# The last feed-forward output as seven block products, with sums made on GpSimd

## The reference, cut to what matters

```python
def swiglu(h, w_in, w_out):
    gate, up = jnp.split(h @ w_in, 2, axis=-1)
    return (jax.nn.silu(gate) * up) @ w_out          # (512, 2816) @ (2816, 1024)

def residual_post_norm(x, y, gate, weight, gain, bias):
    return layer_norm(DN_ALPHA * x + weight * gate[:, None, :] * y, gain, bias)

x = residual_post_norm(x, swiglu(modulate(x, m, 2), ffn2_w_in, ffn2_w_out), m[:, 8], FFN_HALF, ln_gain[2], ln_bias[2])
```

## Time and profile before

| | |
|---|---|
| median of 3 runs | 1345.9 us |
| the profiled execution, its span (first to last instruction) | 1344.9 us |
| the median of the runs over that span | 1.0 us |
| matmuls | 7200 |
| busy share of TensorE, VectorE, ScalarE, GpSimd | 98%, 60%, 38%, 6% |
| mean granted clock of TensorE, as a share of full | 0.995 |

### The profile page before, as it was taken

The page is one execution under the profiler, slowest core; times in us unless marked ns, Lnnn a source line. Parts: engine busy times, 40 slices in busy tenths (PEclk is TensorE's granted clock), DMA queues, the critical chain, the costliest instruction groups (busy, mean ns, idle before and its releaser), DMA issues.

```text
span 1344.9 us, 17714 instructions
## 1 busy us (share of the span) xinstructions
PE 1323.4 (98%) x7200; PEld 1116.1 (83%) x7200; DVE 801.2 (60%) x1146; ACT 517.5 (38%) x718; POOL 74.2 (6%) x83
## 2 busy tenths in 40 slices
PE   8999999999999999999999999999999999999997
PEld 5778888888889999888888788887898888888886
DVE  5546588666777776565136878777863333433356
ACT  5535211222213544566235655556652231222211
POOL 1000000000000000000001111110000000000000
PEclk8999999999999999999999999999999999999999
DMA  9965545665455676552022112123335333333211
GB/s 319 285 177 175 195 151 157 190 186 180 151 178 147 190 188 189 173 172 94 23 79 64 48 48 63 48 64 114 107 85 159 94 103 97 96 101 105 86 63 63
DMA packets 206400, 175.00 MB, mean 130 GB/s; under 512 B 6906, under 2 KB 175464, under 8 KB 206320
## 3 DMA queue, kind: packets, MB, share of 16 engines
q1 hardware_dynamic: 197816, 142.74, 36.6%
q0 software_dynamic: 7808, 29.46, 6.6%
q10 hardware_dynamic: 696, 1.68, 0.4%
HBM read 171.74 MB, written 2.11 MB: 129 GB/s over the span
## 4 chain that ended last, share of the span: by engine, by line
PE 89%; DVE 5%; ACT 3%; issue 2%; DMA 1%; ACTq 0%; DVEq 0%; SPq 0%
PE ps L1962 28%; PE ps L1964 27%; PE ps L1963 27%; PE ps L2001 1%; DVE w_lo L1291 1%; PE ps L2413 1%; PE ps L2398 1%; DMA w_raw<-ffn_w_in 1%; PE ps L2161 0%; PE ps L2014 0%; PE ps L2432 0%; PE ps L2184 0%; DVE xl L1384 0%; DVE xl L1433 0%; PE ps L2205 0%
## 5 line engine op out<-in xcount | busy, mean ns | idle before, releaser
L1962 PE MATMUL ps<-h_hi,w_lo 128*128 128x512 f32 (+1 forms) x1120 | 391.4, 349 | 2.1 <-DVE h_lo L1584 1.0
L1964 PE MATMUL ps<-h_hi,w_hi 128*128 128x512 f32 (+1 forms) x1120 | 387.8, 346 | 0.0
L1963 PE MATMUL ps<-h_lo,w_hi 128*128 128x512 f32 (+1 forms) x1120 | 387.6, 346 | 0.0
L1291 DVE TENSOR_TENSOR w_lo<-w_raw,w_hi 128x2048 fp32r<-128x2048 f32 (+1 forms) x107 | 237.1, 2218 | 169.8 <-ACT w_hi L839 169.7
L839 ACT ACTIVATE w_hi<-w_raw 128x2048 fp32r<-128x2048 f32 (+1 forms) x107 | 198.3, 1854 | 344.9 <-PE ps L1964 315.4
L1962 PEld LDWEIGHTS ps<-h_hi,w_lo 128*128 128x128 f32 x1120 | 211.7, 189 | 32.5 <-issue 5.3
L1964 PEld LDWEIGHTS ps<-h_hi,w_hi 128*128 128x128 f32 x1120 | 211.7, 189 | 26.9
L1963 PEld LDWEIGHTS ps<-h_lo,w_hi 128*128 128x128 f32 x1120 | 211.8, 189 | 25.5
L1313 DVE SCALAR_TENSOR_TENSOR ada_row<-ada_block,c_cols,ada_row 128x256 f32<-128x256 f32 x224 | 108.6, 485 | 8.0
L1462 DVE TENSOR_TENSOR glu<-ps,glu 128x512 f32<-128x512 f32 (+1 forms) x66 | 39.4, 598 | 123.0 <-ACT glu L899 123.0
L1962 PE MATMUL ps<-h_hi,half_lo 128*128 128x512 f32 (+1 forms) x272 | 102.0, 375 | 0.7 <-ACT beside_lo L1123 0.4
(11 more groups left out here) (273 smaller groups left out, 1770.9 us busy)
## 6 DMA issues: line engine op xcount, KB each, us to landing
w_raw<-ffn_w_in SPq DMA_DIRECT2D x124, 512.0 KB, 5.3
w_raw<-ffn_w_out SPq DMA_DIRECT2D x60, 512.0 KB, 4.2
ada_block<-w_ada POOLq DMA_DIRECT2D x28, 1024.0 KB, 5.8
half_raw<-w_mix_in SPq DMA_DIRECT2D x48, 256.0 KB, 3.3
ada_block<-w_ada SPq DMA_DIRECT2D x6, 1024.0 KB, 9.5
w_raw<-ffn_w_in SPq DMA_DIRECT2D x32, 128.0 KB, 6.1
w_raw<-w_mix_in SPq DMA_DIRECT2D x8, 512.0 KB, 4.2
w_raw<-ffn_w_out SPq DMA_DIRECT2D x12, 256.0 KB, 4.1
```

Of the source, the lines that this page charges most:

```text
L1291: nc.vector.tensor_tensor(lo, raw, hi.bitcast(F32), ALU.subtract).then_inc(s_lo[s], 1)
L1962: nc.tensor.matmul(dst, s_low, m_high, start=start, stop=False)
L1963: nc.tensor.matmul(dst, s_high, m_low, start=False, stop=False)
L1964: return nc.tensor.matmul(dst, s_high, m_high, start=False, stop=stop)
```

## The change

The output is a product of 2 x 2 blocks by 2 x 2 blocks: tokens in two halves of 256, the 22 k-tiles in two halves of 11, output columns in two halves of 512. It is made with seven block products (P1 to P7) in place of eight. With left blocks A00, A01, A10, A11 (token half, k half) and weight blocks B00, B01, B10, B11 (k half, column half) the order is P1, P5, P3, P6, P2, P7, P4. Right operands: P1, P3, P2 use B00, B11, B10 as loaded; P5 = B01 + B00, P6 = P5's + B11, P4 = P6's + B10 (`WEIGHT_SUMS`); P7 = B01 + B11. Signs lie in the left operands, sums and differences of token blocks.

- The hidden rows are kept unsplit in `hid_last` (22 x 512 float32); the network has one part of 22 hidden tiles. Each left operand is split when used, by 3 steps of 4, 4, 3 k-tiles a product, into three small slots: `left_high` on ScalarE, `left_low` on VectorE, 256 columns a k-tile.
- GpSimd makes the left sums (11 of 256 columns during the hidden tiles, then 9 steps `left_n2`, `left_s4`, `left_s3`, in place) and the 9 weight sums (`add_beside`), all by `tensor_tensor` from SBUF to SBUF. A raw buffer of P1, P3, P2 is free only when its sum is made too.
- B01 for P5 is loaded on its own by SyncE (`upper_right`), the first step early, the other two after the last hidden product.
- P7's weights: B01 is loaded by SyncE, then GpSimd issues a load of B11 that adds into the same buffer (`add_lower_right`), step s waiting for the high part of step s - 1.
- P1, P6, P7, P4 add up in the same two banks, P5 and P3 in two others. ScalarE copies the banks of P1, P5 and P3 out (`keep`); VectorE joins them with later banks (`join`), multiplies by the gate row and adds to the residual (`add_joined`). P4's first matmul of a tile waits for P7's join of that tile.
- The weights of the last half are not gated any more; the last addition has the gate product ahead of it. The last product has a `LAST_ORDER` of its own.
- Elsewhere several semaphores are merged (the exponentials of the decays into one; the scan mask with the ones; the waits of ScalarE on itself).

```diff
-FFN_PARTS = {"L1": (11, 11), "C": (22,), "L2": (11, 11)}
+FFN_PARTS = {"L1": (11, 11), "C": (22,), "L2": (22,)}
+SEVEN = ("P1", "P5", "P3", "P6", "P2", "P7", "P4")
+SEVEN_STEPS = (4, 4, 3)
+LAST_ORDER = [(0, 0), (0, 1), (1, 0), (2, 0), (1, 1), (2, 1)]
...
             def load(i, pieces=2):
-                if i >= 2:
-                    sp.wait_ge(s_lo[slot_of(i - 2)], USES[i - 2] + 1)
+                before = RAW_USERS[RAW_TURN[i] - 2]
+                sp.wait_ge(s_lo[slot_of(before)], USES[before] + 1)
+                if JOBS[before][1:2] == ("seven",) and JOBS[before][2] in ADDED_BESIDE:
+                    sp.wait_ge(s_wsum, sums_made(*JOBS[before][2:]))
...
+                if key == ("L2", "in", 0, 12):
+                    sp.wait_ge(s_h, PRE["lat", 2, TL - 1] + 1)
+                    upper_right(0)
+                if key == ("L2", "seven", "P1", 1):
+                    last = JOB["L2", "in", 0, 21]
+                    sp.wait_ge(s_done[slot_of(last)], USES[last] + 1)
+                    upper_right(1)
+                    upper_right(2)
...
+            def add_beside(p, s):
+                i = JOB["L2", "seven", p, s]
+                pool.wait_ge(s_loaded[raw_slot(i)], 32 * raw_loads(i))
+                if p == "P1":
+                    pool.wait_ge(s_x[min(s, 1)], 48 if s else 32)
+                else:
+                    split = JOB["L2", "seven", "P5" if p == "P3" else "P6", s]
+                    pool.wait_ge(s_lo[slot_of(split)], USES[split] + 1)
+                    pool.wait_ge(s_wsum, sums_made(p, s) - 3)
+                nc.gpsimd.tensor_tensor(weight_sums[s], weight_sums[s], weights(i)[0], ALU.add).then_inc(s_wsum, 1)
...
+            def left_s4(s):
+                pool.wait_ge(s_left, left_sums("P6", s))
+                pool.wait_ge(s_leftlo, seven_number("P5", s) + 1)
+                nc.gpsimd.tensor_tensor(left("P3", s), left("P2", s), left("P6", s), ALU.subtract).then_inc(s_left, 1)
...
+            def add_lower_right(s):
+                i, (k0, kk) = JOB["L2", "seven", "P7", s], seven_k(s)
+                if s:
+                    pool.wait_ge(s_hi[slot_of(i - 1)], USES[i - 1] + 1)
+                pool.wait_ge(s_loaded[raw_slot(i)], 32 * raw_loads(i))
+                pool.dma_start(weights(i)[0], w2o[:, 11 + k0:11 + k0 + kk, W:D], accum_op=ALU.add).then_inc(s_wacc, 16)
+
+            for j in range(11):
+                pool.wait_ge(s_hf, HID["L2", 0, 11 + j] + 1)
+                nc.gpsimd.tensor_tensor(hid_last[:, j, 256:512], hid_last[:, j, 256:512], hid_last[:, 11 + j, 256:512],
+                                        ALU.subtract).then_inc(s_left, 1)
+            for s in range(3):
+                add_beside("P1", s)
+                left_n2(s)
+            for s in range(3):
+                left_s4(s)
+            for s in range(3):
+                add_beside("P3", s)
+                left_s3(s)
+            add_beside("P2", 0)
+            add_beside("P2", 1)
+            add_lower_right(0)
+            add_beside("P2", 2)
+            add_lower_right(1)
+            add_lower_right(2)
...
+            def left_high(p, s):
+                n = seven_number(p, s)
+                if n == 2:
+                    wait_done(JOB["L2", "in", 0, 21])
+                if n >= 3:
+                    wait_done(SEVEN_FIRST + n - 3)
...
+                for n in range(3 * len(SEVEN)):
+                    p, s = JOBS[SEVEN_FIRST + n][2:]
+                    if n in (3, 6, 9):
+                        keep(SEVEN[n // 3 - 1], 1)
+                    split_both_hi(n + 2)
+                    if n in (2, 5, 8):
+                        keep(p, 0)
...
+            def left_low(p, s):
+                n = seven_number(p, s)
+                dve.wait_ge(s_lefthi, n + 1)
+                hi, lo = left_slot(p, s)
+                nc.vector.scalar_tensor_tensor(out=lo, in0=left(p, s), scalar=left_sign(p), in1=hi.bitcast(F32), op0=ALU.mult,
+                                               op1=ALU.subtract).then_inc(s_leftlo, 1)
...
+                for n in range(3 * len(SEVEN)):
+                    p, s = JOBS[SEVEN_FIRST + n][2:]
+                    before = SEVEN[n // 3 - 1]
+                    if s == 0 and before in ("P6", "P2", "P7") and n:
+                        join(before, 1)
+                        add_joined(before, 1)
+                    split_both_lo(n + 2)
+                    if s == 2 and p in ("P6", "P2", "P7"):
+                        join(p, 0)
+                        add_joined(p, 0)
+                    if n == 16:
+                        for i in range(2):
+                            post_center("lat", 2, i)
+                    if n == 18:
+                        for i in range(2):
+                            post_scale("lat", 2, i)
...
+            def seven_free(p, tile):
+                if p in ("P6", "P3"):
+                    pe.wait_ge(s_kept, (2 if p == "P3" else 0) + tile + 1)
+                if p in ("P7", "P4"):
+                    pe.wait_ge(s_joined, (4 if p == "P4" else 0) + tile + 1)
```

More of the change, by code:

```diff
@@ L8 @@
+import itertools
 from contextlib import ExitStack
@@ L99, in slot_of, with loads_raw @@
     return ((L2_FIRST + 1) % 2, L2_FIRST % 2, 2)[(i - L2_FIRST - 1) % 3] if i > L2_FIRST else 3
+def loads_raw(i):
+    return not (JOBS[i][1:2] == ("seven",) and JOBS[i][2] in WEIGHT_SUMS)
+RAW_USERS = [i for i in range(len(JOBS)) if loads_raw(i)]
+RAW_TURN = {i: n for n, i in enumerate(RAW_USERS)}
+SEVEN_FIRST = JOB["L2", "seven", SEVEN[0], 0]
 USES = [sum(slot_of(j) == slot_of(i) for j in range(i)) for i in range(len(JOBS))]
@@ L146, in out_keys @@
 def out_keys(tag):
+    if tag == "L2":
+        return [(tag, 0, half, i) for half, tiles in ((1, (0, 1)), (0, (0, 1)), (1, (2, 3)), (0, (2, 3))) for i in tiles]
     tiles = TC if tag == "C" else TL
@@ L639, in load @@
                     return
+                if key[1:2] == ("seven",):
+                    (row, half), (k0, kk) = SEVEN_LOADED[key[2]], seven_k(key[3])
+                    for a, b in ((0, 2), (2, kk)):
+                        sp.dma_start(raw[:, a:b, :], w2o[:, 11 * row + k0 + a:11 * row + k0 + b, half * W:(half + 1) * W]
+                                     ).then_inc(s_loaded[s], 16)
+                    return
                 if key[1:2] == ("out",):
@@ L1260, in _ @@
                 high_part(PRE["lat", 2, i])
-            ffn("L2")
-            nc.scalar.preload_act_table_set("sqrt_and_others")
-            for i in range(TL):
-                std_of("post", "lat", 2, i, i + 1)
+            last_ffn()
         @block.vector
@@ new lines, in product_done, with join @@
+            def product_done(p, tile):
+                if tile:
+                    wait_done(JOB["L2", "seven", p, 2])
+                else:
+                    dve.wait_ge(s_seven, SEVEN.index(p) + 1)
+            def join(p, tile):
+                early = {"P6": "P3", "P2": "P1", "P7": "P5"}[p]
+                product_done(p, tile)
+                dve.wait_ge(s_kept, 2 * ("P1", "P5", "P3").index(early) + tile + 1)
+                y = early_sum[early, tile]
+                nc.vector.tensor_tensor(y, y, seven_bank(p, tile), ALU.add if p == "P2" else ALU.subtract
+                                        ).then_inc(s_joined, 1)
@@ L2122, in ffn, with last_ffn @@
+            def last_ffn():
+                for j in range(3, 22):
+                    hidden("L2", 0, j, 0, SEQ)
+                    between("L2", j)
+                for p in SEVEN:
+                    for s, tile in LAST_ORDER if p == SEVEN[-1] else itertools.product(range(3), range(2)):
+                        seven_products(p, s, tile)
             def ffn(tag):
@@ L2131, in ffn @@
                     for half in range(2):
[L2132 to L2135 removed]
+                        b = out_half(tag, part, half, b)
             def between(tag, b):
```

332 lines of the change are left out of this document (223 added, 109 removed).

## The result

The changed kernel took 1389.2 us, the median of 4 runs from 1388.35 to 1390.42; the kernel before, on the same chip, 1345.8 us (4 runs, 1345.26 to 1345.98). The ratio is 1.0323, with an interval from 1.0309 to 1.0338: slower by 43 us. The forecast was 1380, with 1362 to 1400 as the likeliest case and rival B taken in down to 1345.

The account below looks back on a forecast made before the run. TensorE's matmuls were taken to bound the kernel. The terms -15.0 + 27.3 + 14.2 + 5.9 + 1.6 gave +34.0 us on a span of 1344.9, plus 1.0 for the median: 1380, likeliest 1362 to 1400, range down to 1345.

Parts of the forecast that it names:

- rival B: Seven products: exclusion does not hold at these sizes or GpSimd yields; +5 us, 1351, or 1345; chance 0.18.
- rival A: Seven products: the main forecast, GpSimd and VectorE excluding each other plus slow adding loads; 1362 to 1400; chance 0.52.
- rival D: TensorE's clock: stalls between bursts could bring half speed, adding 5 to 20 us, 1385 to 1400; chance 0.14.
- Matmuls, -15.0: Last network's output on TensorE: 462 matmuls in place of 528, same form, 104.7 us for 119.7; gain 15.0 us.
- The exclusion, +27.3: Hidden products' end to P6's last step: GpSimd's sums and VectorE's low parts alternate, stalling TensorE 27.3 us.
- The rate of 2.04 ns a column for GpSimd: GpSimd's two-input sums: rate taken from its 512-column operation, giving 4.18 us for 2048 columns.
- The term without exclusion: P1's third step: late even without exclusion, ready at 14.2 us where TensorE wants it at 10.9; 3.5 us.
- The adding load, +14.2: P7's weights: adding loads taken at 8 us (6 for the third) make its steps 5.8, 5.6 and 2.8 us late.
- P4, +5.9: Before P4: its first matmul waits for VectorE's join of P7, queued behind low parts and post-centres; 5.9 us late.
- the tail, +1.6: After the last matmul: gate product ahead of the last addition, 0.70 us, and VectorE's previous tile 0.9; +1.6 us.
- C: Seven products: no exclusion and an adding load under 4.5 us, started early; -6 us, 1340; chance 0.14.
- The row that spoke for B: Profile before: VectorE's subtraction took 1.23 us beside GpSimd's one-input form, which did not lengthen it.

Follow-up runs that it names:

- e1: Changed kernel with each of GpSimd's 18 sums after the hidden tiles replaced by two fills of its destination, reading nothing: 1365.9 us, ratio 1.0144.
- e7: Kernel before with twelve two-input additions and five one-input products added on GpSimd in the last network, nothing depending on them: 1346.3 us, ratio 0.9999.
- e3: Changed kernel with a semaphore for each adding load, which no longer waits for the previous step's high part: 1390.3 us, ratio 1.0324.
- e5: e3 with GpSimd's last sum with P2's weights before the first adding load, and VectorE's P7 joins ahead of low parts: 1386.3 us, ratio 1.0303.
- e4: Changed kernel with GpSimd's 18 sums after the hidden tiles cut to one column, waits and signals kept: 1361.1 us, ratio 1.0107.
- e8: e6 with the orders of e9 and the nine later left sums moved from GpSimd to VectorE: 1359.9 us, ratio 1.0102.
- e10: e8 with the last three adding loads (P4's weights) replaced by GpSimd additions, and a semaphore for each load of B01: 1365.6 us, ratio 1.0142.
- e9: e6 with P4's adding loads behind P7's, P6's joins around low parts, and output work behind the next low parts: 1364.3 us, ratio 1.0138.
- e6: Changed kernel reordered P1, P5, P3, P6, P7, P2, P4; P6's and P4's weight sums by adding loads, own semaphores, earlier first sum and P6 join: 1359.3 us.

## Why the prediction was right, and where it was short

The sum was +34.0 us on the span; it is 1388.0 - 1344.9 = +43.1. The mechanisms of rival A came, and half clock, which was rival D, came on top of them; the size and its parts, term by term:

- **Matmuls, -15.0.** Right: 7134 of them, at the same pace wherever the clock was full.
- **The exclusion, +27.3.** Right in kind (e1, e7) and near in size. The prediction added up the two engines' work and had P6,2 start 83.1 us after the last hidden matmul; it started at about 84. What the prediction took for stalls alone is 19.6 us of stalls and 8.6 us of the rest, some 6.4 of it at half clock. That the two engines set the pace of this stretch fits GpSimd's timeline, which from 1218.8 to 1283.0 us stands still for 1.0 us in all; that a TensorE at full clock would only have waited longer was not tested. The rate of 2.04 ns a column for GpSimd was low: the first two additions of 2048 columns in the changed kernel, for which it hardly waited, took 4.61 and 4.52 us, 4.18 was taken, and the means are 5.1 to 5.2, with the waiting for VectorE inside. The term without exclusion was added up wrongly: 6.4 + 4.2 + 1.5 + 1.8 is 13.9 and not 14.2, so P1,2 late by 3.0 (e1: 3.2); nothing hangs on it.
- **The adding load, +14.2.** 15.3 measured (6.9, 6.7 and 1.7 for 5.8, 5.6 and 2.8). That they come so near is in part luck. The load's time was mis-sized, 9.5 and 7.7 us where 8 and 6 were taken, inside the bounds of 5.8 and 11.6. And one step of the chain was wrong: P7,1 was put down to the load that waits for the high part of P7,0. By e3 that wait costs P7,1 nothing; it waited for its own plain load, whose buffer was held by GpSimd's sum with P2,2's weights, queued behind a wait. The prediction had not asked what stands behind that wait on GpSimd.
- **P4, +5.9, and the tail, +1.6.** 5.6 and 1.3 (8.9 against 7.6). e5, where the join was moved, took the stall to 2.3, which fits the queue as the prediction had it.
- **The clock.** This is the term that was short: half clock stood at nothing in the sum, as rival D with 0.14, and it came on top of A. D's 1385 to 1400 holds the measured time. The seven stretches hold 34.1 us; with the restarts, TensorE's matmuls took 16.7 us more than at the hidden tiles' pace. Of these 8.6 lie up to P6,2, inside the term above, the other 8 beside P7 and P4. With them the sum is -15.0 + 28.2 + 15.3 + 5.6 + 8.0 + 1.3 = +43.4. That 1380 came within 9 us owes something to luck, since half of what the clock took fell where the prediction had waiting already.
- **The rivals.** B and C fell: VectorE's rows are long, and the adding load takes 9.5 us. The row that spoke for B did not carry over: in e7 a one-input operation shut VectorE out too. e4 tells more: without any sums to speak of on GpSimd the time was 1361, not the 1351 given for B: P7 and P4 stalled for 18.5 us in place of 14.7, and 6.7 us of the rest, for which B had nothing, came with the stalls.

What stays open: how much of e1's 25 us is GpSimd's being less late; why showed no effect of a one-input product and e7 did; and whether P7 can be fed in time with a third raw buffer. None of these was tried.

## What to carry to other kernels

An idle engine is not a free one: before GpSimd is given sums that read SBUF, count VectorE's two-input work in the same stretch and add the two times. A saving on a saturated TensorE is worth its matmuls only if every operand stays ahead; here 40.5 us of stalls brought 16.7 us more, most of it half clock, so a row of stalls cost 1.4 times its length, and 1.3 to 1.8 times in the other runs. Where an engine's queue holds a long wait, list what stands behind it and which buffer that frees.

## What the runs showed that was not expected

- A load that adds 1 MB into SBUF landed in 9.5 us where the plain one from the same queue took 6.9, and its issue took 1.3 us for 0.8. Issued one behind the other, those of 1 MB took 12 to 16 us in e8; three issued some 4 us apart took 8.5 to 10.4 in e10.
- A one-input operation of GpSimd lengthens VectorE's two-input one as well: 4.53 us for 2048 columns and 4.64 for 1536 in e7. A fill does not (2.29 us in e1).
- Moving late work behind urgent work on VectorE took two stalls of 5.1 us away and put 6.2 us on the tail (e9); other stalls came in their place (14.8 us in all, 14.3 in e6).
- Half clock came behind or across seven of the changed kernel's twelve stalls, of 2.0 to 6.9 us; the one of 2.9 us before P5,0 and four shorter ones had none. e8, with no stall from 1235.1 to 1294.1 us, had the full clock from 1240.7 to 1298.7.
